# Row lists of the experts read in a strided order, by two tables of 96 and 64 places

## What is computed

```python
top_val, top_idx = lax.top_k(logits, TOP_K)          # 4 of 32
weights = jax.nn.softmax(top_val, axis=-1)
...
xb = hf[tok]                                         # the rows of one expert
gu = xb @ w_gate_up[e] + b_gate_up[e]                # 1024 x 2048
act = (up + 1.0) * gate * jax.nn.sigmoid(SWIGLU_ALPHA * gate)
return act @ w_down[e] + b_down[e]                   # 1024 x 1024
...
out = jnp.zeros((n_tok, d)).at[row_token].add(y_rows * row_weight)
```

## Time and profile before

| | us |
|---|---|
| median of three runs | 1766.94 |
| lowest and highest run | 1766.47, 1767.54 |
| the profiled execution | 1766.66 |
| its span, first to last instruction | 1764.9 |
| TensorE matmuls busy | 1698.8 (96%) |
| VectorE busy | 1381.7 (78%) |
| ScalarE busy | 1200.8 (68%) |
| POOL busy | 713.1 (40%) |

### The profile page before, as it was taken

One profiled execution on the slowest core, in us unless ns is written; L12 is line 12 of the kernel. 1 busy time (PEld: TensorE's weight loads), 2 busy tenths in 40 slices (PEclk: granted clock), 3 DMA queues, 4 the chain that ended last, 5 costly groups with the idle time before them and its releaser, 6 DMA issues.

```text
span 1764.9 us, 24895 instructions
## 1 busy us (share of the span) xinstructions
PE 1698.8 (96%) x8477; PEld 1346.8 (76%) x8477; DVE 1381.7 (78%) x1048; ACT 1200.8 (68%) x967; POOL 713.1 (40%) x344
## 2 busy tenths in 40 slices
PE   6999999999999999999999999999999999999998
PEld 5878889777888987767767767767767767767776
DVE  4666776755334389999999999999999999999984
ACT  5565555433223368788788788788788788788775
POOL 6124233550000072355465365365365365365110
PEclk9999999999999999999999999999999999999999
DMA  5443343433336469999999999999999999999951
GB/s 177 122 129 85 121 122 107 121 108 119 96 96 231 164 218 397 391 404 392 399 402 392 399 401 392 402 406 388 404 404 391 405 400 398 402 400 395 408 201 49
DMA packets 150865, 504.64 MB, mean 286 GB/s; under 512 B 12733, under 2 KB 73285, under 8 KB 117173
## 3 DMA queue, kind: packets, MB, share of 16 engines
q1 hardware_dynamic: 141652, 478.49, 70.0%
q0 software_dynamic: 9104, 25.28, 6.0%
q10 hardware_dynamic: 48, 0.07, 0.0%
HBM read 487.63 MB, written 20.28 MB: 288 GB/s over the span
## 4 chain that ended last, share of the span: by engine, by line
PE 68%; DVE 14%; issue 9%; ACT 6%; POOL 2%; DVEq 0%; ACTq 0%; POOLq 0%
PE gu_ps L2395 13%; DVE split_l L1928 9%; PE gu_ps L2147 8%; PE gu_ps L2149 8%; PE gu_ps L2148 8%; PE dn_ps L2453 7%; PE gu_ps L2399 7%; PE dn_ps L2459 3%; ACT split_h L1303 3%; PE gu_ps L2409 2%; PE dn_ps L2652 1%; PE gu_ps L2652 1%; PE et_ps L2381 1%; DVE up_sb L1915 1%; PE gu_ps L2169 1%
## 5 line engine op out<-in xcount | busy, mean ns | idle before, releaser
L1928 DVE TENSOR_TENSOR split_l<-ring,split_h 128x2048 fp32r<-128x2048 f32 x384 | 864.8, 2285 | 71.0 <-ACT split_h L1303 69.3
L1303 ACT ACTIVATE split_h<-ring 128x2048 fp32r<-128x2048 f32 x384 | 729.9, 1913 | 113.8 <-PE gu_ps L2399 62.7
L914 POOL COPY icur<-slots 96x1 int32 x30 | 282.8, 9428 | 412.3 <-PE et_ps L2381 410.1
L1536 DVE TENSOR_TENSOR w_lo<-w_raw,w_hi 128x2048 fp32r<-128x2048 f32 (+1 forms) x45 | 104.3, 2318 | 128.8 <-ACT w_hi L1035 122.6
L2409 PE MATMUL gu_ps<-split_l,xgT_h 128*128 128x512 f32 x480 | 139.6, 412 | 17.8 <-DVE split_l L1928 14.0
L2147 PE MATMUL gu_ps<-hT_h,w_hi 128*128 128x512 f32 x392 | 154.6, 394 | 0.6 <-DVE acc L1589 0.6
L2149 PE MATMUL gu_ps<-hT_h,w_lo 128*128 128x512 f32 x392 | 152.7, 390 | 0.0
L2148 PE MATMUL gu_ps<-hT_l,w_hi 128*128 128x512 f32 x392 | 152.6, 389 | 0.0
L2395 PE MATMUL gu_ps<-split_h,xgT_h 128*128 128x512 f32 x512 | 140.6, 396 | 0.9 <-DVE xgT_l L1934 0.9
L2399 PE MATMUL gu_ps<-split_l,xgT_h 128*128 128x512 f32 x512 | 137.2, 390 | 0.0
L2395 PE MATMUL gu_ps<-split_h,xgT_l 128*128 128x512 f32 x512 | 137.2, 390 | 0.0
(11 more groups left out here) (426 smaller groups left out, 3242.1 us busy)
## 6 DMA issues: line engine op xcount, KB each, us to landing
ring<-in_w_gate_up SPq DMA_DIRECT2D x256, 1024.0 KB, 8.0
ring<-in_w_down SPq DMA_DIRECT2D x128, 1024.0 KB, 9.2
w_raw<-in_w_in SPq DMA_DIRECT2D x28, 1024.0 KB, 5.9
arow<-acum_rows POOLq DMA_DIRECT2D x16, 512.0 KB, 6.5
w_raw<-in_w_ssd_out SPq DMA_DIRECT2D x8, 1024.0 KB, 5.4
w_raw<-in_w_in SPq DMA_DIRECT2D x9, 512.0 KB, 6.1
w_raw<-in_w_mix_out SPq DMA_DIRECT2D x4, 1024.0 KB, 7.9
wpg<-in_w_ple_gate SPq DMA_DIRECT2D x2, 2048.0 KB, 19.9
```

Of the source, the lines that this page charges most:

```text
L914: g.tensor_copy(icur[:, :], col).then_inc(idx_done, 1)
L1303: a.activation(split_h[s % SPLIT][:, :], ring[s % RING][:, :], ACT.Copy).then_inc(hi_done, 1)
L1536: v.tensor_tensor(w_lo[RAW_SLOT[n]][:, 0:size], w_raw[RAW_SLOT[n]][:, 0:size], w_hi[HI_SLOT[n]][:, 0:size].bitcast(F32), ALU.subtract).the ...
L1928: v.tensor_tensor(split_l[s % SPLIT][:, :], ring[s % RING][:, :], split_h[s % SPLIT][:, :].bitcast(F32), ALU.subtract).then_inc(lo_done, 1)
```

## The change

The table is no longer read line by line. The columns of the first two experts come as before, in a DMA of their own. The other 30 come in six DMAs of 16 lines each to `slots`, where line 16 b + k goes to place 6 k + b, and once more, the first 64 lines alone, in four DMAs to a second table `slots_half`, where line 16 b + k goes to place 4 k + b. Full experts take their lists from the first table, half experts from the second; the copies on POOL then have 64 partitions for half experts. POOL waits for all 11 DMAs. So the valid rows of an expert stand at intervals over the list, with the empty places between them.

```diff
+SLOT_LOADS = 1 + ROWS // 16 + HALF // 16
...
+        slots_half = here("slots_half", [HALF, NE, 2], I32)
...
             sp.wait_ge(scattered, 16 * CH * TOPK)
-            sp.dma_start(slots[0:ROWS, :, :].rearrange("p e f -> p (e f)"), slot_rows[0]).then_inc(slots_loaded, 16)
+            sp.dma_start(slots[0:ROWS, 0:2, :].rearrange("p e f -> p (e f)"), slot_rows[0, :, 0:4]).then_inc(slots_loaded, 16)
+            for b in range(ROWS // 16):
+                sp.dma_start(slots[b:ROWS:ROWS // 16, 2:NE, :].rearrange("p e f -> p (e f)"),
+                             slot_rows[0, 16 * b:16 * b + 16, 4:2 * NE]).then_inc(slots_loaded, 16)
+            for b in range(HALF // 16):
+                sp.dma_start(slots_half[b:HALF:HALF // 16, 2:NE, :].rearrange("p e f -> p (e f)"),
+                             slot_rows[0, 16 * b:16 * b + 16, 4:2 * NE]).then_inc(slots_loaded, 16)
             sp.wait_ge(x1_stored, 16 * CH)
...
-                g.tensor_copy(icur[:, :], col).then_inc(idx_done, 1)
+                g.tensor_copy(icur[0:rows, :], col).then_inc(idx_done, 1)
...
-                g.tensor_copy(dcur[:, :], col).then_inc(idx_done, 1)
+                g.tensor_copy(dcur[0:rows, :], col).then_inc(idx_done, 1)
...
-                pool.wait_ge(slots_loaded, 16 * j + 16)
+                pool.wait_ge(slots_loaded, 16 * j + 16 * SLOT_LOADS)
...
+                table = lambda rows: slots_half if rows == HALF else slots
+                gather(m0 + 2, table(small)[0:small, column(2), 0], k0 + 3, small)
...
-                def rows_of(e, rows_in, rows_out):
+                def rows_of(e, rows_in, rows_out, rows_next):
 
                     pool.wait_ge(et_done, t0 + e * 2 + 4)
-                    gather(m0 + e + 3, slots[0:ROWS, column(e + 3), 0], k0 + e * 2 + 4, rows_in)
-                    scatter(j * NE + e, slots[0:ROWS, column(e), 0], k0 + e * 2 + 5,
-                            slots[0:ROWS, column(e + 1), 1].bitcast(F32), True, rows_out)
+                    gather(m0 + e + 3, table(rows_in)[0:rows_in, column(e + 3), 0], k0 + e * 2 + 4, rows_in)
+                    scatter(j * NE + e, table(rows_out)[0:rows_out, column(e), 0], k0 + e * 2 + 5,
+                            table(rows_next)[0:rows_next, column(e + 1), 1].bitcast(F32), True, rows_out, rows_next)
```

More of the change, by code:

```diff
@@ L925, in send, with weigh, scatter @@
                                          oob_is_err=False).then_inc(scattered, 16)
-            def weigh(col):
-                g.tensor_copy(wcur[:, :], col).then_inc(w_ready, 1)
-            def scatter(n, col, steps, following=None, landed=True, rows=ROWS):
+            def weigh(col, rows=ROWS):
+                g.tensor_copy(wcur[0:rows, :], col).then_inc(w_ready, 1)
+            def scatter(n, col, steps, following=None, landed=True, rows=ROWS, following_rows=ROWS):
                 pool.wait_ge(y_evac, n + 2)
                 alone(pool)
-                g.tensor_copy(dcur[:, :], col).then_inc(idx_done, 1)
+                g.tensor_copy(dcur[0:rows, :], col).then_inc(idx_done, 1)
                 pool.wait_ge(idx_done, steps)
@@ L942, in scatter @@
                 if following is not None:
-                    weigh(following)
+                    weigh(following, following_rows)
                 if landed:
@@ L973, in one_pass @@
                 small = HALF if isinstance(j, int) else ROWS
-                gather(m0 + 2, slots[0:ROWS, column(2), 0], k0 + 3, small)
+                table = lambda rows: slots_half if rows == HALF else slots
+                gather(m0 + 2, table(small)[0:small, column(2), 0], k0 + 3, small)
                 if isinstance(j, int):
@@ L977, in one_pass @@
                     pool.sem_inc(y_free, 1)
-                def rows_of(e, rows_in, rows_out):
+                def rows_of(e, rows_in, rows_out, rows_next):
                     pool.wait_ge(et_done, t0 + e * 2 + 4)
-                    gather(m0 + e + 3, slots[0:ROWS, column(e + 3), 0], k0 + e * 2 + 4, rows_in)
-                    scatter(j * NE + e, slots[0:ROWS, column(e), 0], k0 + e * 2 + 5,
-                            slots[0:ROWS, column(e + 1), 1].bitcast(F32), True, rows_out)
+                    gather(m0 + e + 3, table(rows_in)[0:rows_in, column(e + 3), 0], k0 + e * 2 + 4, rows_in)
+                    scatter(j * NE + e, table(rows_out)[0:rows_out, column(e), 0], k0 + e * 2 + 5,
+                            table(rows_next)[0:rows_next, column(e + 1), 1].bitcast(F32), True, rows_out, rows_next)
                 if isinstance(j, int):
-                    rows_of(0, ROWS, ROWS)
+                    rows_of(0, ROWS, ROWS, ROWS)
                     with pool.Fori(0, PAIRS - 1) as i:
-                        rows_of(i * 2 + 1, HALF, ROWS)
-                        rows_of(i * 2 + 2, ROWS, HALF)
+                        rows_of(i * 2 + 1, HALF, ROWS, HALF)
+                        rows_of(i * 2 + 2, ROWS, HALF, ROWS)
                 else:
                     with pool.Fori(0, NE - 3) as e:
[L993 to L996, removed]
+                        rows_of(e, ROWS, ROWS, ROWS)
+                for e, rows, after in ((NE - 3, ROWS, small), (NE - 2, small, ROWS)):
+                    scatter(j * NE + e, table(rows)[0:rows, column(e), 0], k0 + NE + e + 1,
+                            table(after)[0:after, column(e + 1), 1].bitcast(F32), not isinstance(j, int) or e < NE - 2, rows, after)
                 if not isinstance(j, int):
```

## The result

| | before | after |
|---|---|---|
| median of the runs, us | 1767.15 | 1775.15 |
| lowest and highest, us | 1766.35, 1767.54 | 1771.22, 1780.68 |
| the profiled execution, its span, us | 1766.66, 1764.9 | 1777.21, 1775.5 |
| TensorE busy, us | 1698.8 | 1701.5 |
| VectorE busy, us | 1381.7 | 1381.7 |

After / before is 1.0045, with a 95% interval of 1.0034 to 1.0056: the change costs some 8 us, where no change was forecast. One of the eight runs after lies far off (1881.41) and is left out of range and ratio, though not of the median, which is 1773.09 without it; the same goes for one run each of E2, E4 and E7. The seven others stand in two groups: four from 1771.22 to 1773.09, three from 1777.21 to 1780.68.

A forecast was written before the change was run, and what follows sets the result against it. TensorE in the dense part and VectorE in the sparse part were taken to bound the kernel. Four terms of 0 on the profiled 1766.66 us, moved to the median, gave 1766.9 us, range 1763.2 to 1770.5.

The forecast's parts named there:

- What bounds the kernel: In the experts, TensorE (dense part) and VectorE (sparse part) set the pace, full for 65.6 of a pair's 66 us.
- Rows spread over the list: 0: Every expert's transfers: busiest DMA engine 0.2 to 0.4 us less; bounds nothing to 7.3 us less, taken as nothing.
- ScalarE's waits for down chunks: Sign of a right forecast: these waits in the experts, 7.3 us, shrink while the time stays.
- The rival at the end of the list: Weight loads beside gathers land 1.0 us later as the last engines carry rows too: up to 1781 us; chance 0.10.
- the faster rival: Weight loads set the pace after all, so up to 7.3 us of ScalarE's waits come back: 1759.6 us; chance 0.08.
- No spread at all: Places dealt singly to DMA engines were spread already; only the ten DMAs remain: 0 to +1.0 us; chance 0.10.
- Copies of 64: POOL's copies in half experts, 64 instead of 96 partitions: nothing either way, with 410.1 us of waiting over them.
- Ten more DMAs on SP, once: Ahead of chunk 10 in SP's queue: 3.7 us (3.3 to 5.8), covered; bounds 0 and +1.0, taken as 0.
- POOL's list, late by the same: Third expert's copy moves from 658.51 to 662.2; rows land by 675.7 or 685.9, wanted at 687.57: covered, 0.

The follow-up runs named there:

- E2: The changed kernel with all eleven table DMAs moved behind the load of chunk 13: 1767.04 us, ratio 1.0001.
- E4: The kernel before with its one table DMA moved behind chunk 15, so POOL's list is late and the weights are not: 1768.43 us, ratio 1.0010.
- E7: The changed kernel with two waits on VectorE, for POOL's copy and for its queue's signal behind the fourth gather: 1771.50 us, ratio 1.0023.
- E1: The changed kernel with its eleven table DMAs kept, but line l going to place l, the old order: 1774.97 us, ratio 1.0044.
- E3: The kernel before with ten added DMAs that nobody reads behind its table DMA: 1771.56 us, ratio 1.0027.
- E6: The kernel before with ten added DMAs that nobody reads ahead of its table DMA, so weights and list are late: 1776.17 us, ratio 1.0041.
- E8: As E7, but VectorE's second wait is for a memset that POOL runs behind the fourth gather's descriptors: 1779.45 us, ratio 1.0068.
- E9: The changed kernel with the same places in the same two tables, filled by three DMAs in place of eleven: 1766.73 us, ratio 0.9995.
- E5: The kernel before with five added DMAs that nobody reads between its table DMA and the chunks: 1768.33 us, ratio 1.0011.

## Why the prediction was wrong

*What bounds the kernel* held: a pair takes 65.79 us after as before, and a transfer that becomes cheaper moves nothing.

*Rows spread over the list: 0* held. Its estimate of 0.2 to 0.4 us off the busiest engine is borne out only in part. The 13 scatters of full experts from the one at 800.88 us on landed after a median of 10.14 us before and of 10.09 to 10.26 in E1 and E3 to E6, which have the old order; with the new order it was 9.78 after the change, 9.83 in E2, 9.79 in E7, 9.30 in E8 and 9.72 in E9. Some 0.35 us, in the shadow of an expert: E2 and E9 end where the kernel before does. The gathers, for which the estimate was made, show none of it: the 14 of full experts in the loop landed after a median of 9.41 us before and of 9.37 to 9.82 in the other runs with the old order, of 9.25 to 9.84 with the new one. Nor do the scatters of half experts (8.33 before, 8.30 in E2, 8.33 in E9). ScalarE's waits for down chunks, which the prediction's signs had shrink, did not: between 740 and 1680 us they are 6.2 before, 9.3 in E2 and 9.9 in E9. The rival at the end of the list and the faster rival are refuted by the times of E2 and E9. No spread at all gives the same time as the forecast, and only the scatters of full experts speak against it. *Copies of 64* cost nothing, as said.

**The step that failed is "Ten more DMAs on SP, once"**, and in it first the size. The price was 0.37 us each from the two small DMAs in view, 3.7, with 5.8 as the most. Measured were 0.63 each and 6.4, above the upper bound. The table's 0.33 was for 96 lines in a row of partitions; 16 lines to neighbouring partitions take 0.42 (E1), 16 lines to every sixth or fourth partition 0.59, plus 0.04 between two of them.

Then the room. The step looked at chunk 14, which had 2.0 us, and let the lateness end with it. With 6.4 us chunk 10, which had landed at 657.20 and was taken at 661.04, is the first that is late, and behind it the loads run at 2.45 us a chunk and recover only 0.3 us with each. In place of "Bounds 0 and +1.0" the step should have had some 4 to 6 us, as E3 has it.

*POOL's list, late by the same*: the sentence "Behind this copy on POOL's queue stands only the next expert's service, which waits for TensorE anyhow" is where the other half was missed. A long copy was priced for the third gather only, where it is covered; there the copy came out short (0.18 us at 664.54). The next service waits for TensorE, but then for VectorE, twice: copy 12.4, descriptors 14.0, rows at 727.1 that TensorE wanted at 722.96. The 10.37 of the earlier trace rows was there to be applied to it.

The Trainium skill (SBUF — State Buffer, section "SBUF: two separate sides") says that GpSimd can't write the descriptors of its DMAs while VectorE runs an operation in a two-port mode. For an operation with two SBUF inputs, which a low part is, that section of the Trainium skill names only a GpSimd operation that reads SBUF as shut out. Here descriptors were held up behind low parts too: 2.73 us with VectorE stopped (E8), 14.02 without (E6). The length differs as well: the same section of the Trainium skill has whoever comes first keep the port for one instruction, and here POOL was kept off over four to six low parts of 2.28 us.

Which boundary between two of VectorE's instructions lets POOL in was not found. In the kernels without added waits, copies that were due 1.37 to 1.69 us ahead of VectorE's next operation that reads `et_ps` came through at it (before, E2, E3, E9), and those that were due earlier, 1.85 to 2.87 us ahead, did not (E5, E1, E6, after) and stood for 9.2 to 12.4 us. The kernels with added waits break this: 2.62 (E7) and 3.12 us (E8) ahead, they came through at it.

The changed kernel's two groups of runs fit this: the lower lies near E3's time, with a quick copy, and the upper near E6's, with a slow one. It was not shown run by run.

## What to carry to other kernels

Price a DMA on a queue by the form of its destination, and follow its lateness past the first late load, to see whether the loads behind it run slower or faster than the work. Ask of each service behind a moved step, not of the first alone, what it will meet at its new time. If a list must be dealt out in a strided order, take the stride on the side of the memory: two DMAs then do the work of ten.

## What was not expected of the hardware

- A hole of 4.2 to 5.1 us on TensorE is followed by a granted clock of 0.50 (1.2 GHz) over the next 3.4 to 6.2 us of its work (after, E1, E6). In E3, with holes of 1.12 us at most, and in E7 it stayed at 1.00 from 660 to 734 us. The length of a hole does not decide alone: one of 2.13 us (after, up to 667.66) left the clock at 1.00, one of 1.94 us (E8, up to 1515.63) was followed by 0.50.
- A semaphore that POOL's queue raises behind an indirect DMA comes before its descriptors are written (E7: VectorE runs past its wait, four low parts from 695.00 on, while the descriptors take until 704.77); one that a memset behind it raises comes after (E8: memset at 698.29, VectorE goes on at 698.44).
- Less waiting can cost time: VectorE, no longer held up by ScalarE (pauses of 0.26 and 0.52 us before, none from 690.84 to 718.80 after), is what kept POOL off.
